# A two-layer decoder trunk in fp32: the first norm folded around its projections, and the attention's PV products taken in pairs of items

## The chip, the cores and the metric

The kernel runs on one core of one Trainium2 chip. The metric is the device time of one execution in microseconds. The kernel before was timed in three runs: median 360.36 us, from 359.83 to 360.83. The profiled execution was a run of its own and took 360.88 us.

## What is computed

The input x is 256 rows of 1024 fp32 numbers. Layer 0 is a sparse attention (NSA) layer, layer 1 a gated linear recurrence (HGRN2), each on a normed input and added to the residual stream, and a last norm ends it. Cut to what the change touches:

```python
h = x * rsqrt(mean(x*x) + eps) * norm_w[0]            # rms_norm, row by row
proj = h @ w_in                                       # 1024 -> q, kc, vc, ks, vs, kw, vw, gates, z
q = rope(q); ks, kw = rope(ks), rope(kw)
k_cmp, v_cmp = compress(kc, pe_k, ..), compress(vc, pe_v, ..)    # silu(blocks @ w1) @ w2
gates = sigmoid(gl)
p_c = masked_softmax(q @ k_cmp); o_c = p_c @ v_cmp
p_s = masked_softmax(q @ ks);    o_s = p_s @ vs       # all blocks are selected at this size
p_w = masked_softmax(q @ kw);    o_w = p_w @ vw
o = gates[0]*o_c + gates[1]*o_s + gates[2]*o_w        # 16 heads of 64, 4 key groups
x = x + (o * silu(z)) @ w_out
```

All products keep fp32 accuracy: a weight or an activation is split into a rounded part (hi) and the rest (lo), and a projection is three products, hi by hi, hi by lo and lo by hi.

## The kernel before

**Weights.** There are 19 units of weight columns (`UNITS`), each 1024 by 512 numbers, 2 MB. The SP queue loads a unit into one of two `raw` buffers (L564, L567); ScalarE (ACT) copies it to `w_hi` (L829, `split_hi`); VectorE (DVE) subtracts and writes `w_lo` (L1040, `split_lo`); TensorE (PE) multiplies. The two raw buffers are refilled when the unit that was in them has been split, and the two hi/lo buffers when its products are done. The order of the first units is KS, KC, KW, Q0, Q1, Z0, Z1. The 2 MB compression matrices `w1k` and `w1v` share one buffer: `w1k` is loaded by SP, `w1v` by ACT's queue after the product that reads `w1k`.

**Order.** One list, `SCHEDULE`, says in which order PE does its steps; the other engines walk the same list and do their part of a step where its last piece stands, so each engine's order is fixed. The weight splits are put into the list by `SPREAD` and `LAG`. Steps named here: `hT` transposes the normed input, `pa` and `pb` are the projections in the two orientations, `stage` transposes roped keys and queries, `cmp1`, `cmpT`, `cmp2` are the compression, `gl` the gate logits, `sc`, `scT`, `pcT` the compressed branch, and in the attention `s` computes scores, `pt` transposes the probabilities of an item, `pv` multiplies them by the values. Eight PSUM banks are reused by `filled`/`drained` semaphores.

**The norm.** For layer 0 the rows are normed first: ACT sums squares (L810), DVE and GpSimd (POOL) multiply x by the row's factor and by `g_row`, the norm weight broadcast over 128 partitions (L1056, L1325, L1328), and only then PE transposes. Everything after, from rope to the gates, reads PSUM as it is.

**The attention.** There are 24 items: a query tile, a key group and two heads each; the first 8 (query tile 0) hold both branches, the last 16 one branch. For an item PE does `s`, DVE the row maximum (L1202), ACT the exponentials (L941), DVE the reciprocals and scales of the item before (L1063, L1068 or L1071), POOL the scaling (L506), PE the four transposes (`pt`, L741), and DVE or ACT copies them to `prob_t`, which has two buffers. Then `pv` has four products, each with 64 columns of values as the stationary side and 128 columns of probabilities moving, all into one half of the PSUM partitions: `o = ps[(g % 2) * HD:(g % 2 + 1) * HD, r * P:(r + 1) * P]`. Items of key groups 0 and 1 go to the lower and upper half, in that order. The PE order is `pt n`, `s n+3`, `pv n-1`. Left-over projection pieces (`filler`) stand behind items 13, 15, 16, 21, 22 and 23.

## Time and profile before

| | us |
|---|---|
| median of three runs | 360.36 |
| profiled execution | 360.88 |
| its span, first to last instruction | 359.0 |
| PE busy | 343.7 (96%) |
| DVE busy | 230.9 (64%) |
| ACT busy | 179.7 (50%) |
| POOL busy | 99.7 (28%) |
| data moved | 49.90 MB, 139 GB/s on average |

By stages, from the table of busy times in chosen stretches (PE busy, in us): 0 to 16, the norm and first transposes: 9.45. 16 to 60: 44.00, with the DMA engines at 100%. 60 to 104: 42.87. 104 to 125.6, the compressed branch: 20.04. 125.6 to 190, the attention: 64.14. 190 to 214: 23.87. 214 to 320, the second layer: 105.97 of 106. 320 to 359, its end and the output: 33.38.

How to read it: a line names an instruction group by the source line that issued it; `L583` is the helper through which all matmuls go, so those are told apart by their tiles. fp32 matmuls outside the hi/lo splits show as two records for one matmul. "PEclk" is the granted share of TensorE's full clock of 2.4 GHz; 0.50 is 1.2 GHz. Ends of matmuls are modelled and longer than their pace, so the pace of a group is read from the starts.

### The profile page before, as it was taken

The page shows a single profiled execution, that of the slowest core. Times are in us where ns is not written, and L with a number is a line of the kernel's source. Part 1 is how long each engine was busy: PE and PEld are TensorE (multiplying, and loading weights), DVE is VectorE, ACT ScalarE, POOL GpSimd, SP SyncE. Part 2 cuts the span into 40 slices and gives each one's busy share as a digit, 9 for nine tenths or more (in the row PEclk, how much of TensorE's full clock was granted, in tenths as well). Part 3 has the DMA queues.
Part 4 walks back from the last instruction along what each step waited for, and adds up shares of the span by engine and source line. Part 5 has one row for each costly group of instructions (what it writes and reads, how often), then busy time and mean ns, then how long its engine had stood idle before and what let it go on. Part 6 is the DMA issues. An engine that isn't in the chain of part 4 may idle for free.

```text
span 359.0 us, 5820 instructions
## 1 busy us (share of the span) xinstructions
PE 343.7 (96%) x2262; PEld 299.7 (83%) x2262; DVE 230.9 (64%) x369; ACT 179.7 (50%) x356; POOL 99.7 (28%) x86
## 2 busy tenths in 40 slices
PE   5699999899999999999999999999999999999993
PEld 4689888788988977788777878999999999889882
DVE  1778792546647678766523870935565997799942
ACT  4561456428455687775613572844663010057721
POOL 3513003314301244564420000003052475543000
PEclk9699999999999999999999999999999999999998
DMA  8999889606469200600510079390666005000111
GB/s 271 392 254 276 307 245 276 184 0 235 112 124 194 42 1 2 214 22 0 196 41 2 1 241 337 130 339 3 233 235 227 8 16 222 0 3 24 37 58 58
DMA packets 28602, 49.90 MB, mean 139 GB/s; under 512 B 3168, under 2 KB 7648, under 8 KB 28576
## 3 DMA queue, kind: packets, MB, share of 16 engines
q1 hardware_dynamic: 25696, 44.36, 39.8%
q10 hardware_dynamic: 2224, 2.62, 2.8%
q0 software_dynamic: 656, 2.56, 2.0%
q8 instruction: 18, 0.29, 0.3%
q14 instruction: 8, 0.07, 0.1%
HBM read 48.49 MB, written 1.05 MB: 138 GB/s over the span
## 4 chain that ended last, share of the span: by engine, by line
PE 81%; DMA 12%; DVE 4%; issue 1%; POOL 1%; ACT 0%; ACTq 0%; DVEq 0%; SPq 0%; POOLq 0%
PE bank L583 74%; DMA w<-in_w1v 6%; DMA raw<-in_nsa 4%; PE bank L741 4%; DMA g_row<-in_norm_w 2%; DVE w_lo L1040 2%; PE bank L628 1%; DVE zT L1056 1%; PE bank L661 1%; POOL prob L506 1%; PE bank L799 0%; DVE prob_t L1214 0%; PE bank L714 0%; PE bank L719 0%; ACTq L532 0%
## 5 line engine op out<-in xcount | busy, mean ns | idle before, releaser
L1040 DVE TENSOR_TENSOR w_lo<-raw,w_hi 128x1024 fp32r<-128x1024 f32 (+1 forms) x84 | 99.4, 1229 | 28.5 <-ACT w_hi L829 28.3
L829 ACT ACTIVATE w_hi<-raw 128x1024 fp32r<-128x1024 f32 (+1 forms) x84 | 76.6, 975 | 9.2 <-DMA raw<-in_nsa 7.2
L583 PE MATMUL bank<-w_hi,h_hi 128*128 128x512 f32 x192 | 78.3, 408 | 0.1
L583 PE MATMUL bank<-w_hi,h_lo 128*128 128x512 f32 x192 | 75.1, 391 | 0.0
L583 PE MATMUL bank<-w_lo,h_hi 128*128 128x512 f32 x192 | 74.9, 390 | 0.0
L583 PE MATMUL bank<-h_hi,w_hi 128*128 128x256 f32 x224 | 63.8, 285 | 0.0
L583 PE MATMUL bank<-h_hi,w_lo 128*128 128x256 f32 x224 | 63.4, 283 | 0.0
L583 PE MATMUL bank<-h_lo,w_hi 128*128 128x256 f32 x224 | 63.4, 283 | 0.0
L506 POOL TENSOR_TENSOR prob<-prob,scl 128x512 f32<-128x512 f32 x24 | 32.5, 1353 | 52.3 <-DVE scl L1068 33.2
L583 PEld LDWEIGHTS bank<-w_hi,h_hi 128*128 128x128 f32 x192 | 36.1, 188 | 9.1 <-issue 2.7
L583 PEld LDWEIGHTS bank<-h_hi,w_hi 128*128 128x128 f32 x224 | 42.9, 192 | 0.2
L583 PEld LDWEIGHTS bank<-h_lo,w_hi 128*128 128x128 f32 x224 | 43.0, 192 | 0.1
L583 PEld LDWEIGHTS bank<-h_hi,w_lo 128*128 128x128 f32 x224 | 43.0, 192 | 0.0
L583 PEld LDWEIGHTS bank<-w_hi,h_lo 128*128 128x128 f32 x192 | 36.0, 188 | 7.9
L583 PEld LDWEIGHTS bank<-w_lo,h_hi 128*128 128x128 f32 x192 | 36.1, 188 | 6.5
L941 ACT ACTIVATE prob<-bank,nmax 128x128 f32<-128x128 f32 (+1 forms) x64 | 26.1, 421 | 12.7 <-DVE nmax L1202 12.6
L583 PEld LDWEIGHTS bank<-qa,kb 128*128 128x128 f32 (+3 forms) x272 | 29.4, 180 | 2.1 <-issue 1.2
L583 PE MATMUL bank<-qa,kb 128*128 128x128 f32 (+3 forms) x272 | 30.0, 265 | 0.0
L583 PE MATMUL bank<-prob_t,v_tok 128*64 128x128 f32 x192 | 26.1, 279 | 0.0
L583 PEld LDWEIGHTS bank<-prob_t,v_tok 128*64 128x64 f32 x192 | 20.3, 136 | 6.1 <-issue 2.3
L1347 POOL TENSOR_TENSOR rp<-rp 128x256 f32<-128x256 f32 (+1 forms) x8 | 9.0, 1123 | 54.7 <-DVE rp L1117 36.9
L1202 DVE TENSOR_REDUCE nmax<-bank 128x2 f32<-128x512 f32 (+1 forms) x24 | 16.4, 687 | 9.0 <-PE bank L583 9.0
(184 smaller groups left out, 448.5 us busy)
## 6 DMA issues: line engine op xcount, KB each, us to landing
raw<-in_hg SPq DMA_DIRECT2D x16, 1024.0 KB, 6.4
raw<-in_nsa SPq DMA_DIRECT2D x12, 1024.0 KB, 12.4
raw<-in_nsa_out SPq DMA_DIRECT2D x8, 512.0 KB, 8.4
raw<-in_hg_out SPq DMA_DIRECT2D x4, 1024.0 KB, 6.2
raw<-in_nsa SPq DMA_DIRECT2D x4, 512.0 KB, 8.7
w<-in_w1k SPq DMA_DIRECT2D x2, 1024.0 KB, 10.8
w<-in_w1v ACTq DMA_DIRECT2D x2, 1024.0 KB, 18.4
g_row<-in_norm_w POOLq DMA_DIRECT2D x2, 512.0 KB, 6.6
```

The costliest lines, as they stand in the source:

```text
L506: nc.gpsimd.tensor_tensor(v(pb_), v(pb_), bc(scl[:, it, 0:nb], 512 // nb, 2), ALU.mult).then_inc(scaled, 1)
L583: return nc.tensor.matmul(o, lhsT, rhs, start=start, stop=stop, skip_group_check=True)
L628: m = nc.tensor.transpose(ps[:, j * P:(j + 1) * P], src[:, c:c + P], ident[:])
L661: m = nc.tensor.transpose(ps[:, c * P:(c + 1) * P].bitcast(FR), stg[:, j % 2, 4 * half + c], ident_r[:])
L741: m = nc.tensor.transpose(ps[:, c * P:(c + 1) * P], prob[:, it % (NS + 1), c * P:(c + 1) * P], ident[:])
L829: m = nc.scalar.activation(dst, src, ACT.Copy)
L941: m = nc.scalar.activation(prob[:, it % (NS + 1), c * w:(c + 1) * w], ps[:, c * w:(c + 1) * w], ACT.Exp, bias=nmax[:, it, c:c + 1], accum_ ...
L1040: m = V.tensor_tensor(lo, src, hi.bitcast(F32), ALU.subtract)
L1056: V.scalar_tensor_tensor(dst, x[:, t], stat[:, nrm, 2, t:t + 1], g_row[:], ALU.mult, ALU.mult).then_inc(sig, 1)
L1202: V.tensor_reduce(nmax[:, it, 0:nb], ps[:].rearrange("p (a b) -> p a b", a=nb), AX.X, ALU.max, negate=True).then_inc(rowmax, 1)
L1347: GP.tensor_tensor(rp[:, 2, 0:w], rp[:, 0, 0:w], rp[:, 1, 0:w], ALU.add).then_inc(r_sum, 1)
```

## The change

1. **Norm around the projections.** x itself is transposed. The norm weight comes as a column: an 8 x 128 load, one small transpose (`gc`) and a copy to `g_cols`. ACT writes `h_hi` as PSUM times `g_cols`, in 16 pieces of 128 x 128, DVE `h_lo`, in between the eighths of the first weight unit (`FIRST_ORDER`). The row factor 1/rms is applied to the results: in the rope instructions and the copy of the values as a scalar; for the transposed projections (kc/vc, gates, z) a row of factors is made by PE (`rs`, two small products of ones and diagonals) and DVE multiplies the PSUM banks in place, before their old readers. Both broadcast loads of `norm_w[0]` and the early one of `norm_w[1]` leave the start; the latter is issued in the attention.
2. **Pairs.** The items are reordered so that key groups 0 and 1 alternate. A `pv` step has one product of 256 columns for each item of a pair; two such halves make a pair, one behind each `pt`. `prob_t` has four buffers, and `oT` is gone (z is multiplied in place).
3. **Arrivals apart.** The second unit's two halves have a semaphore each (`second_in`). The second half of x is loaded by SP between the quarters of the first unit.
4. **Order.** `cmp1 1` stands behind `pa(U_Q0, 1)` and `kcT`, `cmpT 1` behind `pa(U_Q1, 0)`. The split of `wg` (the gate weights) and two small lb operations move from behind the rope of (KS, 1) to behind `pb(U_KC, 1)`. The warm-up matmuls are (5, 1), not (7, 6).

```diff
-IDLE = (7, 6)
+IDLE = (5, 1)
-ITEMS = [(0, gp, 2 * gp + g2, rp, None) for gp in range(2) for g2 in range(2) for rp in range(2)]
-ITEMS += [(1, gp, 2 * gp + g2, rp, b) for gp in range(2) for g2 in range(2) for rp in range(2)
-          for b in range(2)]
+ITEMS = [(0, gp, 2 * gp + g2, rp, None) for gp in range(2) for rp in range(2) for g2 in range(2)]
+ITEMS += [(1, gp, 2 * gp + g2, rp, b) for gp in range(2) for rp in range(2) for b in range(2)
+          for g2 in range(2)]
...
-        if n >= 1:
-            add("pv", n - 1, banks=(ITEM_JOB[n - 1] % 2,))
+        if n >= 2:
+            m = n // 2 - 1
+            add("pv", m, n % 2, banks=(PAIR_JOB[m] % 2,))
         filler(AMONG.count(n))
-    add("pv", NI - 1, banks=(ITEM_JOB[NI - 1] % 2,))
+    for c2 in range(2):
+        add("pv", NPAIR - 1, c2, banks=(PAIR_JOB[NPAIR - 1] % 2,))
...
-                    for c in range(4):
-                        r2, c2 = c // 2, c % 2
+                    c2 = step[2]
+                    for it in pair:
+                        _, _, g, rp_, br = ITEMS[it]
                         vb, kt = (c2, 0) if i == 0 else (br, c2)
-                        r = 2 * rp_ + r2
-                        o = ps[(g % 2) * HD:(g % 2 + 1) * HD, r * P:(r + 1) * P]
-                        m = mm(o, v_tok[:, kt, vb, g], prob_t[:, it % 2, c * P:(c + 1) * P], False, last_of_bank)
+                        o = ps[(g % 2) * HD:(g % 2 + 1) * HD, rp_ * S:(rp_ + 1) * S].rearrange("p (r q) -> p r q", r=2)
+                        probs = prob_t[:, it % 4].rearrange("p (r c q) -> p c r q", r=2, c=2)[:, c2]
+                        m = mm(o, v_tok[:, kt, vb, g], probs, False, last_of_bank)
...
+                elif kind == "rs":
+                    pe.wait_ge(ones_set, 1)
+                    pe.wait_ge(diag_set, TT)
+                    for t in range(TT):
+                        m = mm(ps[:, t * P:(t + 1) * P], ones, diag[:, t], t == 0, t == 1)
...
                     elif key[0:2] == ("pb", U_KC):
                         kv = step[2]
                         wait_full(dve, key)
+                        wait_taken(dve, ("rs",))
+                        if kv == 0:
+                            dve.wait_ge(const_in, 16 * N_CONST)
+                        both = ps[:].rearrange("p (j s) -> p j s", j=2)
+                        V.tensor_tensor(both, both, bc(rs_row, 2, 1), ALU.mult).then_inc(kc_scaled, 1)
+                        dve.wait_ge(kc_scaled, kv + 1)
...
+                        if kv == 1:
+                            dve.wait_ge(wg_hi_d, 1)
+                            V.tensor_tensor(wg_lo[:], wg[:], wg_hi[:].bitcast(F32), ALU.subtract).then_inc(wg_lo_d, 1)
...
+                    elif kind == "pb" and step[1] in (U_Z0, U_Z1):
+                        wait_full(dve, key)
+                        both = ps[:].rearrange("p (j s) -> p j s", j=2)
+                        V.tensor_tensor(both, both, bc(rs_row, 2, 1), ALU.mult).then_inc(z_scaled, 1)
...
-            pool.dma_start(g_row[:], row(t_in["norm_w"][0])).then_inc(g_in[0], 16)
...
-            GP.tensor_tensor(xn[:, 1], x[:, 1], g_row[:], ALU.mult).then_inc(x_w, 1)
-            pool.wait_ge(x_w, 1)
-            pool.wait_ge(rstd, 2)
-            GP.tensor_scalar(xn[:, 1], xn[:, 1], stat[:, 0, 2, 1:2], None, ALU.mult).then_inc(normed_b, 1)
-            pool.wait_ge(normed, 1)
-            pool.dma_start(g_row[:], row(t_in["norm_w"][1])).then_inc(g_in[2], 16)
```

**PE in the attention.** The order of PE around item 4 of the kernel before: transposes, scores with their mask product, and the PV products (`prob_t,v_tok`) of one item.

```order
L741 MATMUL bank<-ident,prob 128x128 x4
L583 MATMUL bank<-k,q 128x256 x4
L583 MATMUL bank<-tri_b,ident_b 128x512
L583 MATMUL bank<-prob_t,v_tok 64x128 x4
L741 MATMUL bank<-ident,prob 128x128 x4
```

The same place after the change, where the two PV products belong to the two items of a pair.

```order
L791 MATMUL bank<-ident,prob 128x128 x4
L611 MATMUL bank<-k,q 128x256 x4
L611 MATMUL bank<-tri_b,ident_b 128x512
L611 MATMUL bank<-prob_t,v_tok 64x256 x2
L791 MATMUL bank<-ident,prob 128x128 x4
```

Four products of 128 columns into one half of the partitions became two of 256 columns into the two halves.

**DVE between unit KW and the rope of (KW, 0).** Before, the last two instructions that take the compressed values from their bank (`zT<-bank,pe_t`) are followed by the split of unit Q0 and the rope.

```order
L1136 TENSOR_TENSOR zT<-bank,pe_t 64x16x16
L1137 TENSOR_TENSOR zT<-bank,pe_t 64x16x15
L1040 TENSOR_TENSOR w_lo<-raw,w_hi 128x1024 x4
L1114 TENSOR_TENSOR rp<-bank,rope 128x256
L1115 TENSOR_TENSOR rp<-bank,rope 128x4x32
L1117 TENSOR_TENSOR rp<-bank,rope 128x4x32
L1118 COPY v_tok<-bank 128x256
```

After, the gate weights' split and the lb operations stand in between; the in-place scaling of the bank (L1228) stands ahead of the eight `zT` instructions.

```order
L1232 TENSOR_TENSOR zT<-bank,pe_t 64x16x16
L1233 TENSOR_TENSOR zT<-bank,pe_t 64x16x15
L1237 TENSOR_TENSOR wg_lo<-wg,wg_hi 128x384
L1238 TENSOR_TENSOR lb<-lbl 128x8
L1240 TENSOR_TENSOR lb<-lbl,lb 128x16
L1103 TENSOR_TENSOR w_lo<-raw,w_hi 128x1024 x4
L1211 SCALAR_TENSOR_TENSOR rp<-bank,stat,rope 128x256
L1212 SCALAR_TENSOR_TENSOR rp<-bank,stat,rope 128x4x32
```

Three instructions moved to here from a place ahead of the first `zT` group. In both orders the four `w_lo` instructions of unit KW stand ahead of the second bank's `zT` group.

**DVE at the start of the attention.** Before, behind the last lb operation and up to the copy of item 0's transposes:

```order
L1195 TENSOR_SCALAR lb<-lb 128x8
L1202 TENSOR_REDUCE nmax<-bank 128x4
L1063 RECIPROCAL rrec<-rsum 128x4
L1068 TENSOR_TENSOR scl<-rrec,gate 128x4
L1040 TENSOR_TENSOR w_lo<-raw,w_hi 128x1024
L1214 COPY prob_t<-bank 128x512
```

After, two of the four z banks are scaled in this stretch (L1247); ACT's reading of those banks now waits for it.

```order
L1304 TENSOR_SCALAR lb<-lb 128x8
L1247 TENSOR_TENSOR bank<-bank,g_row 128x512
L1311 TENSOR_REDUCE nmax<-bank 128x4
L1126 RECIPROCAL rrec<-rsum 128x4
L1131 TENSOR_TENSOR scl<-rrec,gate 128x4
L1103 TENSOR_TENSOR w_lo<-raw,w_hi 128x1024
L1247 TENSOR_TENSOR bank<-bank,g_row 128x512
L1323 COPY prob_t<-bank 128x512
```

The scalings are new rows; the rest kept its order.

## Rows read from the trace of the kernel before

**Rows 1.** Chain of work that ended last: start us, us, what.

```profile
1.24 7.04 DMA g_row<-in_norm_w
...
214.16 105.01 PE bank L583 x786
```

**Rows 2.** Stretches: us; PE, PEld, DVE, ACT, POOL busy (count); PEclk, DMA share, GB/s.

```profile
6.00:7.00 1.00, 0.48 (x3) 0.08 (x1) 0.03 (x1) 0.90 (x3) 0.00 (x0) 1.00 0.96 285
...
9.00:10.00 1.00, 0.00 (x0) 0.00 (x0) 1.00 (x1) 0.00 (x0) 1.00 (x1) 0.50 1.06 410
...
16.00:17.00 1.00, 1.00 (x7) 0.87 (x6) 1.00 (x2) 1.00 (x2) 0.00 (x0) 1.00 1.05 389
...
25.00:30.00 5.00, 5.00 (x29) 4.30 (x28) 5.00 (x4) 1.30 (x2) 1.71 (x2) 1.00 1.12 211
...
35.00:40.00 5.00, 5.00 (x44) 5.00 (x43) 3.48 (x11) 0.34 (x1) 0.00 (x0) 1.00 1.05 387
```

**Rows 3.** Timeline of DVE, 33 to 54 us: start, us, engine, line, tiles.

```profile
33.67 1.34 DVE L1123 TENSOR_TENSOR wg_lo<-wg,wg_hi 128x384 fp32r<-128x384 f32 x1 [1.60 <-ACT wg_hi L871]
...
40.75 4.63 DVE L1040 TENSOR_TENSOR w_lo<-raw,w_hi 128x1024 fp32r<-128x1024 f32 x4 [2.14 <-ACT w_hi L829]
...
53.51 0.42 DVE L1114 TENSOR_TENSOR rp<-bank,rope 128x256 f32<-128x256 f32 x1
```

**Rows 4.** Timeline of ACT, 39 to 60 us.

```profile
39.66 3.90 ACT L829 ACTIVATE w_hi<-raw 128x1024 fp32r<-128x1024 f32 x4 [5.82 <-DMA raw<-in_nsa]
...
59.85 0.28 ACT L896 ACTIVATE hidT<-bank 128x128 f32<-128x128 f32 x1
```

**Rows 5.** Timeline of PE, 28 to 73 us: unit KC's first product, the compression products.

```profile
28.92 0.28 PE L583 MATMUL bank<-h_hi,w_hi 128*128 128x256 f32 x1
...
41.25 3.67 PE L583 MATMUL bank<-w,zT 128*64 128x256 f32 x32
...
60.78 0.66 PE L583 MATMUL bank<-w,hidT 128*128 128x64 f32 x4
...
68.74 3.67 PE L583 MATMUL bank<-w,zT 128*64 128x256 f32 x32 [1.13 <-DMA w<-in_w1v]
```

**Rows 6.** Stretches of 0.05 us of PE with tile w alone (count: records in flight).

```profile
41.25:41.30 0.05, 0.05 (x2) 1.00 1.13 410
...
41.50:41.55 0.05, 0.05 (x4) 1.00 1.31 492
```

**Rows 7.** Timeline of PE, one item of the attention.

```profile
142.41 0.66 PE L741 MATMUL bank<-ident,prob 128*128 128x128 f32 x4
...
143.38 0.28 PE L583 MATMUL bank<-tri_b,ident_b 128*128 128x256 bf16 x1
...
143.59 1.09 PE L583 MATMUL bank<-prob_t,v_tok 128*64 128x128 f32 x8
...
144.61 0.66 PE L741 MATMUL bank<-ident,prob 128*128 128x128 f32 x4
```

**Rows 8.** Timeline of DVE and POOL in the attention.

```profile
137.29 1.04 POOL L506 TENSOR_TENSOR prob<-prob,scl 128x512 f32<-128x512 f32 x1 [1.27 <-DVE scl L1068]
...
143.78 0.68 DVE L1202 TENSOR_REDUCE nmax<-bank 128x2 f32<-128x512 f32 x1
...
144.57 0.16 DVE L1071 TENSOR_TENSOR scl<-rrec,gate 128x2 f32<-128x2 f32 x1
...
172.18 1.23 DVE L1040 TENSOR_TENSOR w_lo<-raw,w_hi 128x1024 fp32r<-128x1024 f32 x1
...
172.18 2.12 POOL L506 TENSOR_TENSOR prob<-prob,scl 128x512 f32<-128x512 f32 x1 [2.60 <-DVE scl L1071]
```

**Rows 9.** Timeline of ACT, 118 to 130 us.

```profile
118.55 0.60 ACT L954 ACTIVATE zT<-bank 128x512 f32<-128x512 f32 x1 [0.46 <-PE bank L583]
...
121.94 0.37 ACT L941 ACTIVATE prob<-bank,nmax 128x128 f32<-128x128 f32 x1 [0.91 <-DVE nmax L1202]
...
129.26 0.37 ACT L941 ACTIVATE prob<-bank,nmax 128x128 f32<-128x128 f32 x1
```

More of the change, by code:

```diff
@@ L98, in schedule @@
     add("idle", 0)
-    for q in range(2):
+    add("gc", banks=(3,))
+    for q in range(4):
         add("hT", 0, 0, q, banks=(4 + q,))
@@ L381, in program @@
         first_in = [sem(f"first_in{q}") for q in range(NQ)]
+        second_in = [sem(f"second_in{half}") for half in range(2)]
         w1_in = [sem(f"w1_in{kv}") for kv in range(2)]
@@ L575, in raw_count @@
         def raw_count(u):
-            return 16 * sum(4 if UNITS[m][0] == "nsa_out" else 2 for m in range(u % NRAW, u + 1, NRAW) if m)
+            return 16 * sum(4 if UNITS[m][0] == "nsa_out" else 2 for m in range(u % NRAW, u + 1, NRAW) if m >= NRAW)
         @block.tensor
@@ L596, in act_ready @@
                 else:
-                    for q in range(2):
+                    for q in range(2 if L else 4):
                         wait_taken(pe, ("hT", L, t, q))
@@ L844, in _ @@
                     ps = bk(key)
-                    if kind == "hT" or kind == "yT":
+                    if step == ("hT", 0, 0, 0):
+                        for what, kk in FIRST_ORDER:
+                            if what == "h":
+                                h0_hi_part(0, kk)
+                            else:
+                                act.wait_ge(first_in[kk // 2], 16)
+                                nc.scalar.activation(w_hi[:, 0, kk], raw[:, 0, kk], ACT.Copy).then_inc(hi_done, 1)
+                    elif step == ("hT", 0, 1, 0):
+                        for kk in range(KT):
+                            h0_hi_part(1, kk)
+                        squares(act, 0, 0)
+                        act.wait_ge(root, 1)
+                        squares(act, 0, 1)
+                        split_hi(1)
+                        nc.scalar.activation(ident_r[:], ident[:], ACT.Copy).then_inc(idents, 1)
+                        nc.scalar.activation(ident_b[:], ident[:], ACT.Copy).then_inc(idents, 1)
+                    elif kind == "yT" or (kind == "hT" and step[1] == 1):
                         t, q = (step[2], step[3]) if kind == "hT" else (step[1], step[2])
```

253 lines of the change are left out of this document (157 added, 96 removed).

## The prediction, made before the changed kernel was run

> **What bounds the kernel now.** I read the page's busy shares first: PE 96% of the span, so the time is PE's work, what comes ahead of it and what comes behind. The chain of waits then shows where it is not: ahead, 7.04 us for the broadcast norm weight, behind which stand the norm and only then PE's transposes; later, PE alone for long stretches such as 105.01 us of the second layer [rows 1]. The change leaves that stretch alone. So it can gain in three places: before PE's projections start, at PE's few waits in the first 75 us, and in the attention from 125.6 to 190 us. The stretch tables give the clock and the DMA rate there, and the timelines the durations.
>
> **Start of the kernel.** Before, PE's warm-up ends between 6 and 7 us, the clock is 0.50 at 9 to 10 and 1.00 again only at 16 to 17 [rows 2], and unit KC's first product is at 28.92 [rows 5]. After, the transposes wait for x alone, which is there at about 5 us, and the first unit is split in eighths. DVE is the slower engine: from about 6.6, 8 pieces of w_lo at 4.63 / 8 = 0.58 us [rows 3] and 8 of h_lo (estimate 0.28 each: a quarter of the 0.68 of a 512-wide operation in rows 8, plus a fixed part) end at about 13.5 to 14. PE needs 2.7 us more for what is then left of (KS, 0) and 5.4 for (KS, 1) (24 products at 0.227), so it is at unit KC at about 21.5, 7.3 us earlier. DVE's split of KC's weights (four more pieces from about 18.2) just keeps up with it. I count nothing of the 7.3 yet, since two things behind it do not move by that much.
>
> First, the DMA. In 35 to 40 us it runs at 387 GB/s, in 25 to 30 at 211 with the engines at 1.12 [rows 2]: it is full, and unit KW lands when all bytes ahead of it have. ACT starts to split KW at 39.66 after a 5.82 us wait for it [rows 4]. What leaves the queue ahead of it is two broadcasts of 0.52 MB, 1.05 MB / 387 GB/s = 2.7 us. So KW lands at about 36.9, not at 33. PE stood there before at 44.85, at the end of the group of 41.25 [rows 5]; it would be there at 37.6, and waits for the first quarter's hi and lo, about 1.1 + 1.2 us (4.63 / 4 and 3.90 / 4 with hand-over), until about 39.3.
>
> Second, DVE. From 40.75 to the rope of (KW, 0) at 53.51 it has no gap: KW's split of 4.63 us, eight zT instructions, Q0's split of as much again [rows 3]. The change adds in this stretch one bank scaling of 128 x 512, as the 0.68 us of 143.78 in rows 8, with its hand-over about 0.75, wg_lo 1.34 [rows 3] and the lb operations 0.35: 2.45 us. Its start moves by 2.7. The rope of (KW, 0) comes at 53.51 - 2.7 + 2.45 = 53.3. And wg_lo, at about 48.3, holds `gl`, which PE reaches at 45.5: 2.8 us of idle PE. Behind the rope hangs ACT's order (stage 2's hi part, two bank copies, two table loads, gT, hidT), which ended with hidT at 59.85 [rows 4]; it now ends about 0.2 earlier, so `cmp2` stands at 60.0 and not at 60.78 [rows 5]. Of 7 us of early start 0.8 is left. All terms below are counted from here.
>
> Then PE's wait of 1.13 us for w1v [rows 5] goes, since that product stands one unit later and its load is issued about 2.7 us earlier: +1.1. Moving `cmp1 1` and `cmpT 1` changes no amount of work. The two rs products and the small transpose fall into idle PE. First part: 1.9 us gained. Its bounds: 0, if PE at half clock behind the 2.8 us of idling eats it; 4.5, if KW lands 2 us earlier still (its bytes are through about 2 us before it is signalled, some DMA engines lag, and what makes them lag may have been the two GpSimd broadcasts) and DVE's additions are smaller.
>
> **PV in pairs.** One item's PV takes 1.02 us from its first record at 143.59 to the next transposes at 144.61 [rows 7]: 8 records at 0.107 = 0.85, and 0.17 around them. All go to one half of the array's columns. The kernel has the other case too: `cmp1` alternates halves and has 32 records of 256 columns. One such record alone streams twice as long as one of 128, 0.213 us, so 32 would take 6.8 us; the group takes 3.67 [rows 5], and the table of 0.05 us stretches has two records in flight from the first moment on, four only from 41.50 [rows 6]. So neighbours in different column halves run beside each other. A half step after the change has 4 records of 256 columns: 2 x 0.213 = 0.43, plus the 0.17, 0.60 us. Saved: 1.02 - 0.60 = 0.42 a step, 24 steps: 10.1 us. Without overlap 4 x 0.213 = 0.85 and nothing is saved; that is the lower bound.
>
> The Trainium skill (TensorE: Matmul & The Clock Gate, "The mechanism") says that matmuls start and end strictly in program order, whatever tile they use. By that rule a step's second record, the same item's second pass, blocks the other item's first, and a step would take 3 x 0.213 + 0.17. Rows 6, with two in flight at once, speak against it, but only the counts do; it is a rival below. The skill (TensorEngine Tiling (Array Packing), "PSUM Bottleneck") also warns that column tiling speeds up TensorE and not the evacuation; that is what comes next.
>
> **What the attention gives back.** An item would pace at 2.20 - 0.42 = 1.78 us (2.20 is 142.41 to 144.61). Its chain: mask product of s(n) at 143.38, row maximum at 143.78, scales at 144.57, POOL from 0.24 later and 1.04 long [rows 7, 8], so the transposes of n-1 can start 2.6 us after the mask's start. PE now gets there in 0.21 + 0.60 + 1.78 = 2.6: just in time. Where DVE splits a weight at the same moment POOL needs 2.12, not 1.04 [rows 8], and PE waits about 0.9. Eight of L1040's instructions lie in this stage; two are behind fillers of 1.4 us and two at its start, so 4 x 0.9 = 3.6 is given back. Bounds: 0 to 6.
>
> At the stage's start the z bank that ACT read at 118.55 is now scaled first, and DVE does that behind the lb operations, just ahead of the row maximum for which ACT's exponentials of 121.94 waited 0.91 us [rows 9]. Everything behind it in ACT's order follows: that read, a weight split, a p_ct copy, the exponentials of item 2 (those of 121.94). ACT's idle gaps take some of this; I put item 3's exponentials (129.26) 1.4 later and the transposes behind them 1.2 later [rows 9]. The first three transposes have no PV between them, so PE has nothing to hide it with. Bounds 0 and 2.5. Attention: 10.1 - 3.6 - 1.2 = 5.3.
>
> **Hidden edits.** Four prob_t buffers: copies were waited for only at job starts; nothing counted. z in place, the late load of norm_w[1] (needed some 15 us after it is issued; DMA mostly idle): nothing. Rope with a scalar operand: same elements, same durations, 0. If each of its 28 instructions cost 0.05 more, it would be mostly hidden, 0.2 on the path.
>
> **Sum.** 360.9 - 1.9 - 5.3 = 353.7 for a profiled execution; the median stands 0.5 below that execution, so about 353.
>
> **Rivals.**
> *A. Passes in order.* A step takes 0.81, saves 0.21, 5.1 in all; PE is then slower than the chain, so only the 1.2 is given back: 3.9. 360.4 - 1.9 - 3.9 = 354.6, and 356 if half of POOL's waits stay. For it: the rule; against: rows 6.
> *B. The small terms come out well.* KW lands at 35 (3.8 gained ahead), POOL's waits are covered by fillers and buffers (10.1 - 1.5): 360.4 - 3.8 - 8.6 = 348. For it: the lag is unexplained, and chain times are read from DVE's order with its present gaps.
> *C. No overlap at all in short bursts*, since each burst is fenced by full-width products: nothing saved in PV, 1.2 lost, 1.9 gained: 359.7, within the noise. Against: two in flight at the first moment.
> *D. The clock (slower than before).* PE gets waits it did not have: 1.7 us ahead of KW, 2.8 ahead of `gl`, 1.4 ahead of `cmp2`, some at the attention's start. Before, PE fell idle at about 6.5 us, was at 0.50 by 9 to 10 and at 1.00 again at 16 to 17 [rows 2]: up to 7 us at half speed, worth 3.5 each. From the third such stretch on the gain of 7.2 is gone: with three, 360.4 - 7.2 + 10.5 = 363.7. For it: the 2.8 us wait is longer than the idle time at which the clock fell. Against: the others are shorter and PE is full between them; one stretch would mostly be hidden by the slack ahead of `cmp2`.
>
> **Chances.** Forecast 0.52 (own range 350.5 to 356), A 0.16, B 0.18, C 0.06, D 0.06, the rest 0.02. A measurement of this kernel tells about 0.3% (1.1 us) from no change. Faster: the forecast, A, B and a part of C: 0.89; same: most of C, 0.04; slower: D and the rest, 0.07. The range takes in B's and A's values: 347.5 to 358.
>
> **What would show it.** PE's first w_hi product near 8 us; KW's hi split at 36 to 37.5; PE idle ahead of the first product of KW and 2 to 3 us ahead of `gl` with `wg_lo` as its releaser; `cmp2` within 1.5 us of 60; no wait for w1v. In the attention PV steps of 0.60 us to the next transposes (0.81 is rival A, 1.02 is C), PE waiting for POOL where DVE splits weights, and the transposes of items 2 and 3 late. Wrong would be: `cmp2` before 57 (then the DMA or DVE argument fails), or the clock column below 1.00 after 17 us.

## The result, and the profile after

The changed kernel takes 357.57 us (median; 356.34 to 359.01), 0.9927 [0.991, 0.9944] of the kernel before: 2.6 to 2.8 us faster, where 7.4 were forecast. Before, executions lay within 1 us (of 25 later ones, all but one from 359.9 to 361.3); now they spread over 2.7, and the profiled one (356.69 us, span 354.2) is one of the two shortest, so its trace shows less than the median lost. One execution among all the runs, the profiled one of e17 (376.75 us), ran at a mean clock of 0.85; neither its time nor its trace is used below.

The page after, busy shares, the granted clock in 40 slices, and the chain by engine:

```profile
PE 332.1 (94%) x2157; PEld 281.1 (79%) x2157; DVE 233.6 (66%) x396; ACT 181.8 (51%) x372; POOL 89.7 (25%) x83
...
PEclk9999989999999999999999999999999999999999
...
PE 66%; DVE 13%; ACT 8%; DMA 7%; issue 3%; POOL 1%; SPq 1%; DVEq 0%; ACTq 0%
```

PE was 343.7 us busy and is 332.1 now, 11.6 less, but the span is 4.8 shorter: most of what PE saved came back as waiting, and PE's share of the chain fell from 81% to 66%. One digit of the clock is an 8, near 50 us. The second layer's long stretch is unchanged and starts 4.85 us earlier (209.31 and not 214.16 [rows 1]).

The stretches of the changed kernel (columns as in [rows 2]):

```profile
48.00:49.00 1.00, 0.80 (x7) 0.83 (x8) 0.96 (x4) 0.79 (x1) 0.00 (x0) 0.95 1.07 368
49.00:50.00 1.00, 1.00 (x7) 0.91 (x6) 1.00 (x2) 0.00 (x0) 0.00 (x0) 0.50 1.07 287
...
52.00:53.00 1.00, 1.00 (x10) 0.96 (x8) 0.97 (x2) 0.00 (x0) 0.00 (x0) 0.84 1.14 252
...
125.60:190.00 64.40, 56.62 (x349) 37.48 (x348) 40.37 (x90) 41.09 (x132) 26.51 (x23) 1.00 0.22 74
```

From 48.9 to 52.3 us the clock is at 1.2 GHz (0.50), behind two waits. And in the attention PE is busy for 56.62 of 64.40 us, where it was for 64.14.

PE's timeline: KW's first product, `gl`, `cmp2`, then the attention.

```profile
40.03 0.47 PE L611 MATMUL bank<-w_hi,h_hi 128*128 128x512 f32 x1 [2.32 <-DVE w_lo L1103]
...
48.20 0.29 PE L611 MATMUL bank<-h_hi,wg_hi 128*48 128x256 f32 x1 [1.84 <-DVE wg_lo L1237]
...
59.84 0.41 PE L611 MATMUL bank<-w,hidT 128*128 128x64 f32 x2 [0.31 <-ACT hidT L957]
...
123.17 0.60 PE L791 MATMUL bank<-ident,prob 128*128 128x128 f32 x4
...
128.64 0.66 PE L791 MATMUL bank<-ident,prob 128*128 128x128 f32 x4 [2.56 <-DVE prob_t L1323]
...
132.67 0.65 PE L611 MATMUL bank<-prob_t,v_tok 128*64 128x256 f32 x4
133.25 0.65 PE L791 MATMUL bank<-ident,prob 128*128 128x128 f32 x4
```

The first three rows are the front. The last two answer to [rows 7]: a PV half takes 0.58 us to the next transposes, where an item took 1.02. PE's waits in the attention, by releaser (us in total, times, longest):

```profile
PE bank L791 <- ACT prob_t L991: 3.0, 4, 1.1
PE bank L791 <- DVE prob_t L1323: 2.8, 2, 2.6
PE bank L791 <- POOL prob L532: 2.2, 3, 0.9
```

That makes 8.0 us; before there were none in this stretch. The names say who came last, not why. For that, here is what one weight split does, on all engines:

```profile
143.34 1.05 ACT L882 ACTIVATE w_hi<-raw 128x1024 fp32r<-128x1024 f32 x1
144.28 0.59 ACT L991 ACTIVATE prob_t<-bank 128x512 f32<-128x512 f32 x1
144.42 1.22 DVE L1103 TENSOR_TENSOR w_lo<-raw,w_hi 128x1024 fp32r<-128x1024 f32 x1 [1.82 <-ACT w_hi L882]
144.93 0.66 PE L791 MATMUL bank<-ident,prob 128*128 128x128 f32 x4 [0.95 <-ACT prob_t L991]
...
145.57 0.68 DVE L1311 TENSOR_REDUCE nmax<-bank 128x2 f32<-128x512 f32 x1
...
146.34 0.47 ACT L1002 ACTIVATE prob<-bank,nmax 128x256 f32<-128x256 f32 x1 [1.47 <-DVE nmax L1311]
...
147.26 0.59 ACT L991 ACTIVATE prob_t<-bank 128x512 f32<-128x512 f32 x1
...
147.91 0.66 PE L791 MATMUL bank<-ident,prob 128*128 128x128 f32 x4 [1.13 <-ACT prob_t L991]
```

ACT's half of the split stands ahead of a copy that PE waits 0.95 us for. DVE's half stands ahead of a row maximum; the exponentials wait 1.47 for that, the next copy stands behind them in ACT's order, and PE waits another 1.13. One split, 2.1 us. At another place it is POOL that is late:

```profile
152.77 1.22 DVE L1103 TENSOR_TENSOR w_lo<-raw,w_hi 128x1024 fp32r<-128x1024 f32 x1
152.93 3.09 POOL L532 TENSOR_TENSOR prob<-prob,scl 128x512 f32<-128x512 f32 x2 [1.27 <-DVE scl L1134]
...
155.03 0.63 PE L791 MATMUL bank<-ident,prob 128*128 128x128 f32 x4 [0.89 <-POOL prob L532]
```

Two of POOL's products, 1.04 us each elsewhere, take 3.09 beside DVE's w_lo, and PE waits 0.89 us: this is the wait that the forecast described. The start of the attention, on ACT:

```profile
123.37 1.28 ACT L1012 ACT_TABLE_LOAD   x1
124.66 0.60 ACT L1012 ACTIVATE zT<-bank 128x512 f32<-128x512 f32 x1
125.16 0.62 ACT L1015 ACTIVATE zT<-zT 128x512 f32<-128x512 f32 x1
125.68 1.05 ACT L882 ACTIVATE w_hi<-raw 128x1024 fp32r<-128x1024 f32 x1
126.74 1.28 ACT L1002 ACT_TABLE_LOAD   x1
128.04 0.37 ACT L1002 ACTIVATE prob<-bank,nmax 128x128 f32<-128x128 f32 x1
```

From 123.37 on, for 4.7 us, no exponential is made, and DVE's w_lo for this split (126.76 to 127.98) stands ahead of the copy that PE waits 2.56 us for. Before, the first item's PV (2.0 us with its opening product) lay in this gap; in pairs it needs item 1's transposes copied, and comes behind the transposes of item 2.

### The profile page after: what moved, and what is told of

It reads as the page before. It is cut to its first block, busy times and chain, and to the rows that moved or that the text cites. A ratio compares the mean times of both kernels' runs of the same rounds, so it can differ in the third digit from the quotient of the medians.

```text
span 354.2 us, 5694 instructions
## 1 busy us (share of the span) xinstructions
PE 332.1 (94%) x2157; PEld 281.1 (79%) x2157; DVE 233.6 (66%) x396; ACT 181.8 (51%) x372; POOL 89.7 (25%) x83
## 3 DMA queue, kind: packets, MB, share of 16 engines
HBM read 47.97 MB, written 1.05 MB: 138 GB/s over the span
## 4 chain that ended last, share of the span: by engine, by line
PE 66%; DVE 13%; ACT 8%; DMA 7%; issue 3%; POOL 1%; SPq 1%; DVEq 0%; ACTq 0%
PE bank L611 62%; DMA raw<-in_nsa 7%; DVE w_lo L1103 5%; PE bank L791 2%; ACT w_hi L882 2%; ACT prob L1002 1%; DVE nmax L1311 1%; POOL prob L532 1%; PE bank L711 1%; ACT h_hi L889 1%; DVE prob_t L1323 1%; ACT w_hi L908 1%; PE bank L852 0%; DVE zT L1232 0%; DVE zT L1233 0%
## 5 line engine op out<-in xcount | busy, mean ns | idle before, releaser
L1103 DVE TENSOR_TENSOR w_lo<-raw,w_hi 128x1024 fp32r<-128x1024 f32 (+1 forms) x80 | 93.1, 1207 | 39.8 <-ACT w_hi L882 39.8
L611 PE MATMUL bank<-w_hi,h_hi 128*128 128x512 f32 x192 | 77.0, 407 | 3.0 <-DVE w_lo L1103 2.3
L882 ACT ACTIVATE w_hi<-raw 128x1024 fp32r<-128x1024 f32 (+1 forms) x80 | 72.7, 971 | 12.4 <-DMA raw<-in_nsa 10.5
L532 POOL TENSOR_TENSOR prob<-prob,scl 128x512 f32<-128x512 f32 x24 | 27.9, 1164 | 56.2 <-DVE scl L1131 35.6
L1447 POOL TENSOR_TENSOR rp<-rp 128x256 f32<-128x256 f32 (+1 forms) x8 | 9.3, 1168 | 66.0 <-DVE rp L1214 48.9
L791 PEld LDWEIGHTS bank<-ident,prob 128*128 128x128 f32 x96 | 10.5, 140 | 15.8 <-ACT prob_t L991 8.6
L791 PE MATMUL bank<-ident,prob 128*128 128x128 f32 x96 | 15.3, 282 | 8.0 <-ACT prob_t L991 3.0
L1030 ACT ACTIVATE z_hg<-bank 128x512 f32<-128x512 f32 x4 | 2.4, 597 | 36.2 <-PE bank L611 36.2
```

The costliest lines, as they stand in the source:

```text
L532: nc.gpsimd.tensor_tensor(v(pb_), v(pb_), bc(scl[:, it, 0:nb], 512 // nb, 2), ALU.mult).then_inc(scaled, 1)
L611: return nc.tensor.matmul(o, lhsT, rhs, start=start, stop=stop, skip_group_check=True)
L791: m = nc.tensor.transpose(ps[:, c * P:(c + 1) * P], prob[:, it % (NS + 1), c * P:(c + 1) * P], ident[:])
L882: m = nc.scalar.activation(dst, src, ACT.Copy)
L1103: m = V.tensor_tensor(lo, src, hi.bitcast(F32), ALU.subtract)
L1447: GP.tensor_tensor(rp[:, 2, 0:w], rp[:, 0, 0:w], rp[:, 1, 0:w], ALU.add).then_inc(r_sum, 1)
```

## Experiments

The idea that I began with (theory 1) was that the two parts add up, and that the attention fell short because all transposes share PSUM bank 7. The rivals were POOL's chain and the clock. "Waits" below are PE's between the first transposes and the last PV.

**The parts alone.** e1 puts PV back; e2 puts only the new PV (with z in place) into the kernel before.

```diff
-        if n >= 2:
-            m = n // 2 - 1
-            add("pv", m, n % 2, banks=(PAIR_JOB[m] % 2,))
+        if n >= 1:
+            add("pv", n - 1, banks=(ITEM_JOB[n - 1] % 2,))
```

> The changed kernel with PV as before: items in their old order, PV item by item behind the next item's transposes, two buffers for the transposed probabilities. What is left of the change is the start of the kernel and the scaling of the z projections. The trace of the changed kernel shows the attention starting 2.5 us earlier than before. Theory 1 (the two parts add up, and the attention is the one that fell short): 360.4 - 2.5, and up to 0.7 back for the start of the attention: 357.9 to 358.6. Theory 2 (the front gives more than its 2.5 us and the new PV nothing, or less than nothing): 357.6 or below, as fast as the changed kernel. Theory 3 (low-clock stretches of some executions, brought by PE's new idle time in front, eat the front's gain): median 358.5 or more, with a spread of over 2 us between its own executions.

> The kernel before with the new attention alone: items in pairs, PV halves between the transposes, four buffers, z in place. The front is the old one. Theory 1: the attention gives 2.3 us, as the two traces show from the first transposes to the last PV: 358.1, and slightly better (357.6) if the z scaling at its start cost 0.5. Theory 2 (PV in pairs is worth nothing): 360.2 to 360.6. The forecast's term (10.1 saved, 3.6 given back, and no z scaling here) would give 353.9. Theory 3 (clock): a spread below 1.2 us, as that of the kernel before, since PE's idle time in front is the old one.

e1: 359.46 (359.09 to 361.36; ratio 0.9979 [0.9953, 1.0005]), two of seven executions at 361. e2: 357.92 (356.55 to 359.21; 0.9931 [0.9906, 0.9956]), three at 356.5 to 356.9 and three at 359. So the front is worth only about 1 us, and the PV pairs give 2.5 by the ratio and 3.8 in the three short executions, not 2.3: from the first transposes to the last PV the profiles have 63.1 us before, 59.8 in e2, 64.3 in e1. e1's median and spread are those of its theory 3, but not for that reason: with unused products in PE's waits the front alone has the same median (e15 below, 359.43). The expectation on e2's spread failed: the new low-clock executions come with the pairs too. One more thing: e2 has the old front, but its first transposes are at 124.68 and not at 125.69. The wait for w1v of [rows 5] isn't there. So the old front does not always have it; these are one trace of each kernel.

**Two banks for the transposes** (e3).

```diff
-        add("pt", n, banks=(7,))
+        add("pt", n, banks=(3 if n % 2 and 1 < n < 22 else 7,))
```

> The changed kernel with one number different: the transposes of the odd items 3 to 21 go to PSUM bank 3, which nothing else uses there, and the others stay in bank 7. Theory 1 (the transposes of an item wait for the copy of the item before out of the one bank, and the shorter PV no longer hides that copy): of some 8 us of PE waits among the items about half go, 3 to 4.5 us: 353.5 to 354.5. Rival (the chain of scores, row maximum, scales and POOL's scaling ends last, and the copy is merely the wait that the profile names): within 0.5 us of the changed kernel, 357 to 358, with POOL named as the releaser in place of the copies.

358.58 (357.25 to 360.65), 0.9953 [0.9934, 0.9972]; no gain. The waits in e3:

```profile
PE bank L791 <- POOL prob L532: 5.3, 4, 2.0
PE bank L791 <- DVE prob_t L1323: 2.8, 2, 2.6
```

The 3.0 us for ACT's copies are gone, and POOL's went from 2.2 to 5.3: 8.1 in all. The bank was not the cause; the rival was right in naming the chain. (The profiled execution was the longest of the twelve, 360.65 us, which lost 3.4 us of clock behind the start's wait and 1.7 at 151 to 155 us.)

**The splits in the chain** (e5: both halves of the splits among the items cut to 8 of 512 columns; e11: DVE's half alone. The expectations speak of six splits; the traces show seven cut, the quarter at the start of the attention among them).

```diff
+            if (u, q) in SMALL:
+                sl = slice(2 * q, 2 * q + 2)
+                return [(w_hi[:, u % 2, sl, 0:8], raw[:, u % NRAW, sl, 0:8], w_lo[:, u % 2, sl, 0:8])]
```

> The changed kernel with the six weight splits that stand among the items (units 7 and 8, w_hi on ACT and w_lo on DVE) cut to 8 of 512 columns each; the rest of those weights isn't split, so part of the computation is left out. Nothing else moves. Theory (a step of 1.77 us gives the scores, which are issued three steps ahead, 5.3 us instead of 6.6; their chain of row maximum, exponentials, scales and POOL's product takes about 4.1 us, and a split of 1.2 us on DVE or 1.05 us on ACT in front of one of its instructions is more than what is left): PE's waits in the attention, 8.0 us, fall to 3 or less, and an execution takes 351.5 to 353. Rival 1 (the chain is too long without any split): waits of 6 us or more stay, 355 or above. Rival 2 (the one bank of the transposes): the waits for POOL go, those for the copies, 5.8 us with the start, stay: 354.5.

> As the run with six small weight splits, but only DVE's half of each split, w_lo, is cut to 8 of 512 columns; ACT splits w_hi in full. A part of the computation is left out by that. Theory (both halves stand in the chain, DVE's 1.22 us ahead of row maximum and scales, ACT's 1.05 ahead of exponentials and copies): between the two, waits of 4 to 5 us in the attention and 352.8 to 354.5. If DVE's half alone does it: waits of 2 us, 350.7. If ACT's alone: waits of 7 or more, 356 to 357.

e5: 350.66 (350.23 to 351.3), 0.9729. The waits in e5:

```profile
PE bank L796 <- DVE prob_t L1328: 1.5, 2, 1.3
PE bank L796 <- POOL prob L534: 0.2, 1, 0.2
PE bank L796 <- ACT prob_t L996: 0.2, 1, 0.2
```

8.0 us became 1.9, and the stretch from the first transposes to the last PV 6.0 us shorter (54.8 and not 60.8). The time is below the 351.5 to 353 that was expected. Neither the bank nor the chain is too long without the splits: it is the splits. e11: 354.01 (352.89 to 354.55), waits 4.5 us, as expected: DVE's half has 3.5 of the 6, ACT's the rest. DVE's 3.5 hold two things that no run separates, w_lo's place in DVE's order and POOL's slowness beside it: in e11 every product of POOL in the attention takes 1.04 or 1.42 us, where the changed kernel has up to 3.09 for two.

**More look-ahead** (e6; e12 adds a late slice of z and a later split).

```diff
-NS = 3
+NS = 4
...
-        s_c = sb("s_c", [P, TT, 512], F32, att)
+        s_c = prob_t[:, 0:2]
```

> The changed kernel with scores four items ahead instead of three: five buffers for the probabilities, and PSUM bank 3 as a fourth bank for scores from item 6 on; the compressed branch's score tiles lie in the buffers of the transposed probabilities, to make room. Everything is computed. Theory (the slack of the chain is what lacks): each item gains 1.77 us of slack, so the waits for POOL go, and those for copies become short; waits 8.0 to about 2.5 us, 351 to 353 in an undisturbed execution, median below 354, and fewer low-clock stretches. Rival (ACT and DVE are short of time, not of look-ahead, or the one bank of the transposes decides): above 355.

> Everything that the runs pointed to, with all of the computation: the changed kernel with scores four items ahead (five buffers for the probabilities, bank 3 as fourth score bank from item 12 on), the last slice of the z projections behind the scores of item 5 instead of ahead of the first transposes, and the second quarter of unit 7 split later. Theory (with one more item ahead the waits among the items outside the start fell from 5.2 to 1.8 us, and the start's waits, which grew to 4.1, stand behind two table loads, silu and one split in ACT's order, which now come behind the exponentials of items 3 to 5): waits in the attention below 3 us, 351.5 to 353 in all executions, faster than both kernels. Rival (the silu and its table loads only fall into later items and hold those up by as much, 3.8 us on ACT): 355 to 357.

e6: 357.93 (356.29 to 358.3). Outside the start the waits fell from 5.2 to 1.8 us as expected, but those of the start grew from 2.8 to 4.1, and the clock fell twice:

```profile
58.00:60.00 2.00, 0.67 (x5) 0.60 (x5) 0.36 (x1) 1.99 (x4) 0.72 (x1) 0.95 1.15 191
60.00:62.00 2.00, 2.00 (x7) 1.71 (x7) 0.81 (x5) 2.00 (x5) 1.28 (x1) 0.50 1.06 295
62.00:64.00 2.00, 2.00 (x7) 1.58 (x7) 1.93 (x4) 1.01 (x2) 0.00 (x0) 0.70 1.05 345
...
130.00:132.00 2.00, 0.00 (x0) 0.00 (x0) 0.99 (x4) 2.00 (x13) 0.57 (x1) 0.87 0.00 0
132.00:134.00 2.00, 1.99 (x9) 1.90 (x10) 1.49 (x4) 1.70 (x10) 1.51 (x2) 0.50 0.00 0
134.00:136.00 2.00, 2.00 (x7) 0.67 (x6) 0.94 (x3) 0.89 (x7) 0.48 (x1) 0.78 0.00 0
```

e12: 356.47 (355.0 to 357.73): no wait at the third transposes, but 3.30 us at those of item 5, where the silu, its table loads and two splits now stand. Both missed what was expected.

**The column halves** (e7).

```diff
-ITEMS = [(0, gp, 2 * gp + g2, rp, None) for gp in range(2) for rp in range(2) for g2 in range(2)]
-ITEMS += [(1, gp, 2 * gp + g2, rp, b) for gp in range(2) for rp in range(2) for b in range(2)
-          for g2 in range(2)]
+ITEMS = [(0, gp, 2 * gp + g2, rp, None) for gp in range(2) for g2 in range(2) for rp in range(2)]
+ITEMS += [(1, gp, 2 * gp + g2, rp, b) for gp in range(2) for g2 in range(2) for b in range(2)
+          for rp in range(2)]
```

> The changed kernel with items ordered so that both items of a pair write the same half of the columns, as two products that follow each other did before; sizes, counts, buffers and places of the PV halves are the same. Theory (what shortens PV is that neighbours run beside each other in different column halves): a half step takes about 1.02 us instead of 0.58 to the next transposes, and the attention is as long as before: 359.5 to 360.5. Rival (the longer product of 256 columns in place of two of 128, that is fewer instructions, shortens it): steps of 0.6, 356.3 to 357.6.

364.22 (362.92 to 365.81), 1.0091 [1.0073, 1.0109]. A PV half in e7:

```profile
154.08 1.08 PE L611 MATMUL bank<-prob_t,v_tok 128*64 128x256 f32 x4
155.09 0.66 PE L791 MATMUL bank<-ident,prob 128*128 128x128 f32 x4
```

1.01 us, against 0.58 with two halves of the columns: what shortens PV is that neighbours run beside each other. The stretches of PE with tile v_tok alone show it too. In the 0.1 us in which such a group starts, two records are in flight in the changed kernel (first row), one in e7 (second row).

```profile
132.60:132.70 0.10, 0.03 (x2) 1.00 0.00 0
154.05:154.15 0.10, 0.07 (x1) 1.00 1.06 410
```

e7 isn't as fast as before but 0.9% slower: the first PV comes later (the same 2.55 us ahead of the third transposes), and the clock falls behind that (128 to 135 us at 0.50). e7 also has the long step back with every split in its place: PE's waits among the later items are 1.2 us, where the changed kernel has 5.2.

**The z scaling** (e8) **and a later split** (e9: one number of a table).

```diff
-                        act.wait_ge(z_scaled, 2 * (u - U_Z0) + m2 + 1)
+                        wait_full(act, key)
...
-                        V.tensor_tensor(both, both, bc(rs_row, 2, 1), ALU.mult).then_inc(z_scaled, 1)
```

> The changed kernel with the scaling of the z projections by 1/rms left out (four DVE products of 128 x 512), which is a part of the computation; ACT reads these banks as soon as PE has filled them. Theory (the scaling in front of ACT's reads delays what the first items wait for, by the 1.2 us that were forecast and that the front alone lost between its first transposes and its last PV): the wait of 2.56 us ahead of the third transposes falls by 1.0 to 1.3, an undisturbed execution takes 355.2 to 355.5. Rival (that wait comes from the split and the silu in ACT's order and not from the scaling): 356.2 to 356.6 as now.

> The changed kernel with the split of the second quarter of unit 7 moved from the place between the first items' transposes to one behind the transposes of item 3; nothing else moves by more. Theory (the 2.56 us ahead of the third transposes are the copy of item 1 behind this quarter's w_lo, which waits for its w_hi): that wait falls to about 1.3 us, as it did where the split was cut small, part of the gain comes back as a wait of about 0.5 at the new place, 355.5 to 356.2 in an undisturbed execution, and the low-clock stretch behind that wait, 2.2 us in the executions that have it, comes less often: median 356.5. Rival (the wait is the table loads and silu in ACT's order, and moves only its name): wait of 2.3 or more, 357 to 358 in the median.

e8: 357.05 (355.77 to 359.22); the wait ahead of item 2 is 1.82 and not 2.56, a fall between the two expectations. e9: 358.39 (356.99 to 360.46), slower than the changed kernel. PE in e9:

```profile
128.40 0.63 PE L791 MATMUL bank<-ident,prob 128*128 128x128 f32 x4 [0.73 <-POOL prob L532]
...
131.86 0.63 PE L791 MATMUL bank<-ident,prob 128*128 128x128 f32 x4 [0.69 <-POOL prob L532]
...
139.88 1.09 PE L791 MATMUL bank<-ident,prob 128*128 128x128 f32 x4 [2.45 <-POOL prob L532]
```

The start's wait went, and came back as 2.45 us at item 6, where this split meets the next one, with a fall of the clock. My expectation had 0.5 there. The traces of e8 and e9, and that of e1, show one more thing in the front: with the wait ahead of KW (1.96, 2.29 and 2.10 us) alone, the clock falls within 1.5 us of its end. In e8:

```profile
40.00:42.00 2.00, 2.00 (x7) 1.55 (x6) 2.00 (x3) 1.76 (x4) 0.00 (x0) 0.58 0.61 223
```

PE is slower then and reaches `gl` 1.6 us later, so the wait there is 0.2 and not 1.8. In e8 and e9 the clock falls again at 61 us, and their first transposes are at 124.48 and 124.77; in e1 it does not, and they are at 123.20.

**The clock** (e4: unused products ahead of unit KW and `gl`; e10: also ahead of the first `cmp2` and of the transposes of item 2).

```diff
+WARM = {("pa", 2, 0, 0): 9, ("gl",): 7, ("cmp2", 0): 5, ("pt", 2): 9}
...
+                    for _ in range(WARM[step]):
+                        mm(bank[2 if kind == "pt" else 3][:], h_hi[:, 0, 0:P], h_hi[:, 0:2].rearrange("p k s -> p (k s)"), True, True)
```

> The changed kernel with products that nothing uses in PE's two new idle places: nine of 128 x 512 ahead of unit KW's first product (2.0 us) and seven ahead of gl (1.6 us). No work is taken away. Theory 3 (the idle time of 2.3 and 1.8 us makes the clock fall, for 3 to 4 us in the profiled execution, and for longer or a second time in the slower executions): the clock stays at 1.00 in 49 to 52 us, the spread falls from 2.7 to about 1 us, and the median from 357.6 to about 356.3. Rival (the low clock there is hidden, and the spread has another cause): 357.3 to 357.9 with the same spread.

> The changed kernel with products of 128 x 512 that nothing uses in all four idle places: nine ahead of unit KW, seven ahead of gl, five ahead of the first cmp2, nine ahead of the transposes of item 2. No work is taken away and no wait of another engine changes. Theory (two levels of one kernel are low-clock stretches behind PE's idle time, at about 60 us, worth 1.4, and at about 128 us, worth 2.2): the granted clock is 1.00 from 17 us to the end of the attention, all executions lie within 1 us, at 356.2 to 356.9, median 356.5 against 357.6. Rival (PE's idle time is not what lowers the clock, or other products lower it too): two levels as before, a median of 357.5 or more.

e4: 358.24 (355.87 to 360.05), nothing gained. The clock no longer fell at 49 us but, behind 0.43 and 1.29 us of waiting for ACT, at 60 us, where nothing hides it: the first transposes are at 124.65, against 123.06 in e10. e10: 355.89 (355.76 to 356.0), 0.9876 [0.9863, 0.9889]: 1.7 us less for thirty more products of 0.23 us that nobody uses, and all executions within 0.24 us. The same places in e10:

```profile
48.00:50.00 2.00, 1.96 (x17) 1.98 (x18) 1.99 (x3) 0.72 (x1) 0.00 (x0) 1.00 1.07 345
60.00:62.00 2.00, 2.00 (x11) 1.70 (x11) 0.75 (x5) 2.00 (x6) 1.29 (x1) 1.00 1.06 279
128.00:130.00 2.00, 1.51 (x11) 1.32 (x11) 1.57 (x5) 2.00 (x13) 0.08 (x1) 1.00 0.00 0
```

**Sizes with the clock held** (such products in front, and in the attention where the wait is).

> The front of the change alone, with PV as before, and the three groups of unused products in front. Theory (the front's own worth is what the traces show up to the first transposes, 2.5 us, less what the start of the attention gives back, 1.2): 360.3 - 1.3 = 359.0, tight, and no execution at 361 as two had without these products. Forecast's terms: 360.4 - 1.9 + 1.2 = 359.7. If the clock cost the front alone nothing: 359.5, as without them.

> The changed kernel without the scaling of the z projections (left out of the computation), with the three groups of unused products in front and six ahead of the transposes of item 2, so that no low-clock stretch blurs the difference. Against the 355.89 of the changed kernel with such products: theory (the scaling costs the forecast's 1.2 on the path): 354.7. Rival (it costs about 0.7, as the wait fell from 2.56 to 1.82): 355.2. If nothing: 355.9.

> Scores four items ahead, as in the run with that name, and unused products in PE's idle places: nine ahead of unit KW, seven ahead of gl, five ahead of the first cmp2, fourteen ahead of the transposes of item 2, where that kernel waited 3.56 us. All of the computation is done. Theory (the look-ahead did save waits, 3.9 us from the first PV to the last, and what hid it were 1.3 us more of waiting at the start and the low-clock stretches): 355.9 - 3.9 + 1.3 = 353.3, range 352.8 to 354, all executions within 1 us. Rival (the look-ahead's gain is an artefact of where PV starts): 355.5 to 356.3, as the three-ahead kernel with these products.

> The version with scores four ahead, the late slice of z and the later split, with nine, seven and five unused products in front and twelve ahead of the transposes of item 6, where it waited 3.30 us. All of the computation is done. Theory (clock falls cost that version 1.5 to 3): 353.2 to 353.9, tight. Rival (PE waits elsewhere bring the clock down all the same): 355 to 357 with a spread of 2.

e15 (front alone): 359.43 (359.17 to 359.71), 0.9974 [0.9963, 0.9985]. The clock cost the front alone nothing in the median. e16 (without z scaling): 355.15 (354.83 to 355.55), 0.9854, as its rival said. e13: 353.87 (353.62 to 354.15), 0.9819 [0.9806, 0.9831], everything computed, the fastest full version of all. Its waits:

```profile
PE bank L800 <- ACT prob_t L1000: 1.8, 4, 0.9
PE bank L800 <- DVE prob_t L1332: 0.9, 2, 0.5
```

So the look-ahead is worth 2.0 us once the clock stays up; the rest of the start's wait (14 x 0.23 = 3.2 us) is filled, not removed. e14: 358.2 (357.8 to 359.1), a miss of mine. PE in e14:

```profile
136.28 0.66 PE L800 MATMUL bank<-ident,prob 128*128 128x128 f32 x4 [3.29 <-DVE prob_t L1332]
...
138.52 4.11 PE L614 MATMUL bank<-h_hi 128*128 128x512 f32 x12
```

The wait is at item 5, and the products stood ahead of item 6: they filled nothing, ran at half clock up to 140.9 us and held the next transposes back by 3.95 us (138.52 to 142.47). e18 puts them ahead of item 5; e17 adds to e13 the later split (and six products, not fourteen).

> As the run with the late slice of z and twelve products ahead of the transposes of item 6, but fourteen of them ahead of item 5's, which is where the wait of 3.3 us stands; behind item 6's they cost their whole time. Theory (a stretch at half clock behind that wait cost 1.5 to 2): 353.2 to 354, tight, about as the version with the slice in its old place. Rival (something else in this order costs more): above 355.

> The version with scores four ahead and unused products, and beside it the second quarter of unit 7 split behind the transposes of item 3 (the two quarters behind it each two places later), with six products instead of fourteen ahead of the transposes of item 2, since its wait is shorter then. Theory (the start's 3.6 us of idle PE are that split's 1.05 and 1.22 us as well as the table loads; with four items ahead the split finds room later): 353.9 - 1.3 = 352.6. Rival (the split only moves the wait, as it did with scores three ahead, where 0.7 became 2.45 us at item 6): 353.5 to 355 with a low-clock stretch near 138 us.

e18: 356.67 (355.66 to 356.83): 1.5 better than e14, so the place was the fault, but a wait of 1.86 us at item 7 is left, with a fall of the clock behind it in the profiled execution; three of five ran at a mean clock of 0.990, at 356.7 to 356.8, and two at 0.998, at 355.7 to 355.9. e17: 354.54 to 354.92, slower than e13 by 0.8 (by the ratios) to 1.0; where it waits no trace shows. Neither run that moves this split alone (e9, e17) gains by it; with everything computed, the start's wait was only ever filled or moved.

## Why the prediction was wrong

Set against each other, in us gained, from the ratios with the clock held (each 1% is 3.6 us; a difference of two ratios is good to about 0.7 us):

| Term | Forecast | Measured | From |
|---|---|---|---|
| front, up to the attention | 1.9 | 1.7 | e15: 0.9, and the z scaling |
| z scaling at the attention's start | -1.2 | -0.8 | e16 against e10 |
| PV steps shorter | 10.1 | 10.3 | 24 x (1.01 - 0.58) |
| waits of PE in the attention | -3.6 | -6.8 | what is left of e10 against e15 (3.5 in all) |
| clock | 0 | -1.8 | changed kernel against e10 |
| sum | 7.2 | 2.6 | 0.9927 |

The -6.8 agrees with the traces: the changed kernel waits 8.0 us, e15 waits 1.2.

**Start of the kernel: right.** KW's hi split begins at 37.57 us (forecast 36.9), its first product is at 40.03 (39.3), the rope of (KW, 0) at 52.91 (53.3), `cmp2` at 59.84 (60.0). Within this, wg_lo took 0.56 us and not 1.34, and the 1.1 us for w1v were no gain of the change, since e2 hasn't that wait either. Of 7.3 us of early start 0.9 arrived at `cmp2`, as argued (0.8). That the whole term came out near 1.9 is partly luck: 1.1 of it was the w1v wait, and against e2, which hasn't it, e10's first transposes are 1.6 us earlier (123.06 and 124.68).

**PV in pairs: right.** 0.58 us a step against a forecast of 0.60, and e7 shows the column halves as the cause; rival A (0.81, by the order rule of the Trainium skill, TensorE: Matmul & The Clock Gate, "The mechanism") and rival C are out: by that rule the orders of e7 and of the changed kernel would differ by 0.21 us a step, not by 0.43.

**What the attention gives back: this step failed.** I took the chain of one item at its undisturbed durations, found it "just in time", and charged 0.9 us at four places because POOL is slower beside a DVE split. That happens, at one place clearly (0.89 us at 155.03); and L1040 stands seven times in this stage, not eight. The splits' own time in the orders of DVE and ACT (1.22 and 1.05 us, ahead of row maxima, exponentials and copies) was charged nothing, though it was in the rows. The look-ahead of three items was worth 3 x 2.20 = 6.6 us and became 3 x 1.77 = 5.3; that 1.3 us was what had hidden one split. Without the splits the waits fall from 8.0 to 1.9 (e5); those among the later items fall from 5.2 to 1.8 with more look-ahead (e6), and to 1.2 with the long steps back (e7). The measured 6.8 are two sums: about 1.9 at the start (2.8 of waits there, against 0.9 with PV item by item in e1), where I saw that no PV stands between the first three transposes, but not that the first PV's 2 us had lain in a wait and were moved out of it; and about 5.0 among the later items.

**The clock: the rival that I gave 0.06 took 1.8 us, though not its sign.** I priced a stretch at 3.5 us and wanted three for a loss. The stretch that I expected (ahead of `cmp2`) is hidden as I said. But one near 60 us costs 1.6 (e4's first transposes against e10's), one behind the start's wait about 2 (in e6's trace 2 x 0.13 + 2 x 0.50 + 2 x 0.22 = 1.7 us of clock are lost, in those of e3 and e7 3.4; e2's two levels lie 2.3 apart), and they come in some executions only; so the median moved, by as much as the front gives. The longer executions of the changed kernel itself have no trace: that these stretches are what they lost is inferred from e10 and from their mean clock (0.983 to 0.988, against 0.993), not seen.

What stays open: 2.4 to 3.0 us lie outside the span in three of the five executions of the changed kernel, in all six of e6 and of e7, and in some of e3, e5, e8, e9, e11 and e12, against 1.7 to 1.9 in every one of before, of e1 and e2 and of all kernels with unused products. No view shows where. It isn't the 1.8 above: the spans alone differ by as much (median 355.8 in the changed kernel, 354.05 in e10). And why the same wait of 2.56 us lowers the clock in one execution (e3, e7) and not in another (the changed kernel's profile) was not found, and no run tried it.

## What to carry to other kernels

When a step of a pipeline gets shorter, the look-ahead, counted in steps, gets shorter in time: list for each engine everything that can stand in the chain's way for one step, weight preparation included, and compare the longest with the slack that is lost (here 6.6 - 5.3 = 1.3 us, against splits of 1.05 and 1.22). Then look at what the saved work was hiding in: work that fills a wait saves nothing by being shortened or moved. And after a change that gives PE new waits, compare the spread and the clock of several executions before explaining the median; products that nobody uses in those waits are a cheap test, and here brought 1.7 us.

## What the runs showed of the hardware

- fp32 products (two records each) in different column halves run beside each other: four records of 256 columns in 0.58 us to the next instruction, against 1.01 in one half (e7).
- The same instruction, wg_lo over 128 x 384, took 1.34 us in [rows 3] (and in e2) and 0.56 in its new place (and in e1). In the trace of before a product of POOL (33.30 to 34.59) ran beside it, in the changed kernel POOL was idle (for 23.95 us up to 53.99); no run separates that from other causes.
- POOL's product over 128 x 512 took 1.04 us in most places, 2.12 beside w_lo in [rows 8] and 1.95 in the changed kernel (157.40, with w_lo from 157.24); with w_lo cut to 8 columns (e11) it never took more than 1.42 in the attention.
- The clock went to 1.2 GHz behind waits of 2.3 and 1.8 us (changed kernel), behind one of 2.0 to 2.3 us alone (e1, e8, e9), and behind 0.43 and 1.3 us near 60 us in e4, where the earlier ones were filled, in e6, where it had not fallen behind them, and in e8 and e9, where it had; in e1 it stayed up behind the same 0.43 and 1.3. It is back after 3 to 7 us in the traces read. With all four places filled (e10) it was at 2.4 GHz from 2 to 208 us.
